# Six chunks of gathered rows among the one-hot groups, and another order of the embedding units

## The reference, cut to what matters

```python
hf = rms_norm(x, norm_ffn)
x = x + peer_ffn(hf, ...)      # 8 heads x 16 chosen experts of 16384 for each token
x = x + jax.nn.sigmoid(rms_norm(x, ple_norm) @ ple_w_gate) * (pe @ ple_w)
```

## Time and profile before

| | |
|---|---|
| median of 3 runs | 4200.87 us (4199.17 to 4205.4) |
| the profiled execution | 4196.88 us |
| its span | 4194.8 us |
| TensorE, VectorE, GpSimd busy | 89%, 63%, 44% of the span |
| data moved | 1063.93 MB, a mean of 254 GB/s |
| layer 0: one-hot groups, dense pairs, end | from 930, 1036 and 1957 us |
| layer 1: the same | from 3019, 3123 and 4046 us |

### The profile page before, as it was taken

One profiled execution on the slowest core, in us unless ns is written; L12 is line 12 of the kernel. 1 busy time (PEld: TensorE's weight loads), 2 busy tenths in 40 slices (PEclk: granted clock), 3 DMA queues, 4 the chain that ended last, 5 costly groups with the idle time before them and its releaser, 6 DMA issues. The chain is left out here.

```text
span 4194.8 us, 42902 instructions
## 1 busy us (share of the span) xinstructions
PE 3743.3 (89%) x15498; PEld 2766.4 (66%) x15498; DVE 2647.2 (63%) x5548; ACT 734.3 (18%) x1375; POOL 1860.7 (44%) x1714
## 2 busy tenths in 40 slices
PE   8889998978999999994797899989789999999937
PEld 7546787867666666651685467878676666666516
DVE  4766215748677676877657652167486777668776
ACT  2243302212000000000222433022120000000002
POOL 6101103776455455556371020047664554555563
PEclk9889999999999999997898999999899999999968
DMA  3201134548999999999722011445599999999997
GB/s 104 111 30 41 57 137 115 125 120 299 409 409 409 409 402 410 406 409 397 274 83 111 31 41 67 141 119 123 131 311 410 409 406 407 409 408 407 402 391 267
DMA packets 333955, 1063.93 MB, mean 254 GB/s; under 512 B 79152, under 2 KB 96176, under 8 KB 312496
## 3 DMA queue, kind: packets, MB, share of 16 engines
q0 software_dynamic: 184320, 537.08, 34.8%
q1 hardware_dynamic: 132368, 505.22, 31.9%
q10 hardware_dynamic: 17056, 18.88, 1.3%
HBM read 1025.27 MB, written 35.78 MB: 253 GB/s over the span
## 5 line engine op out<-in xcount | busy, mean ns | idle before, releaser
L1665 PE MATMUL bank<-v_tile,shared 128*128 128x512 f32 x2048 | 908.4, 598 | 38.5 <-DVE shared L2041 35.3
L2100 POOL DMA_INDIRECT u_rows<-in_peer_u,idx_all x512 | 645.1, 1260 | 591.9 <-DVE act_u L1998 478.2
L2010 DVE SCALAR_TENSOR_TENSOR x<-v_rows,act_w,x 128x1024 f32<-128x1024 f32 x512 | 657.7, 1285 | 335.2 <-DMA v_rows<-in_peer_v,idx_all 316.9
L2100 POOL DMA_INDIRECT v_rows<-in_peer_v,idx_all x512 | 561.7, 1097 | 423.4 <-DVE x L2010 331.7
L1998 DVE CUSTOM_DVE_ANT_0 u_rows<-u_rows,h 128x1024 f32<-128x1024 f32 x512 | 610.9, 1222 | 189.9 <-DMA u_rows<-in_peer_u,idx_all 187.5
L1665 PEld LDWEIGHTS bank<-v_tile,shared 128*128 128x128 f32 x2048 | 392.5, 192 | 493.1 <-issue 447.2
L2110 POOL DMA_INDIRECT first_cells<-first_gate,cell_all x256 | 417.1, 1629 | 578.5 <-DVEq L1990 462.4
L1653 PE MATMUL bank<-hT,bT 128*128 128x256 f32 x2048 | 452.5, 379 | 0.0
L1653 PEld LDWEIGHTS bank<-hT,bT 128*128 128x128 f32 x2048 | 388.4, 190 | 72.0 <-issue 22.0
L1557 PE MATMUL bank<-hT,ring 128*128 128x256 f32 x1536 | 341.1, 383 | 14.2 <-PEq L150 14.2
L1557 PEld LDWEIGHTS bank<-hT,ring 128*128 128x128 f32 x1536 | 293.6, 192 | 56.5 <-issue 15.8
(11 more groups left out here) (375 smaller groups left out, 4749.8 us busy)
## 6 DMA issues: line engine op xcount, KB each, us to landing
v_tile<-in_peer_v SPq DMA_DIRECT2D x256, 512.0 KB, 7.5
ring<-in_w_in_panels SPq DMA_DIRECT2D x76, 1024.0 KB, 4.9
bT<-in_peer_ut SPq DMA_DIRECT2D x128, 512.0 KB, 7.9
ring<-in_peer_w_query SPq DMA_DIRECT2D x32, 1024.0 KB, 5.2
aT<-in_peer_ut SPq DMA_DIRECT2D x64, 512.0 KB, 6.9
sT<-in_peer_ut SPq DMA_DIRECT2D x64, 512.0 KB, 6.8
ring<-in_ple_w_gate SPq DMA_DIRECT2D x24, 1024.0 KB, 6.8
first_cells<-zeros SPq DMA_DIRECT2D x16, 1024.0 KB, 11.1
```

Of the source, the lines that this page charges most:

```text
L1665: ins = mm(acc[t][part][:, :], act_pair[p % AHEAD][:, at:at + P], v_tile[:, e % DENSE, part * 512:part * 512 + 512], start=(e == 0), stop= ...
L2010: stt(out=m.x[:, 2 + t, :], in0=vr[:, n % RINGS, :], scalar=act_w[:, p % 4, i:i + 1], in1=m.x[:, 2 + t, :], op0=ALU.mult, op1=ALU.add).the ...
L2100: nc.gpsimd.indirect_dma_start(out=rows[:, n % RINGS, :], out_offset=None, in_=table, in_offset=bass.IndirectOffsetOnAxis(ap=idx_all[:, t, ...
```

## The change

`HOT_CHUNKS` goes from 4 to 6: chunks 0 to 5 lie behind one-hot groups 4, 9, 14, 19, 24 and 29, each with the `pre` that stood there now behind it; `query(1, 2)` moves with chunk 3 to group 19. Chunks 6 to 8 lie beside `pre(6)` to `pre(11)`. `DENSE_END` goes from 59 to 61, so the 64 pairs are spread over chunks 9 to 60, again 52 chunks. The units run in the order 1, 0, 2. The end of the list becomes

```diff
-HOT_CHUNKS = 4
+HOT_CHUNKS = 6
-DENSE_END = 59
+DENSE_END = 61
+LOADS_AT = 59
+SUMMED_AT = 65
...
-    after = {DENSE_END: [("add",), ("embed", 0)], DENSE_END + 1: [("scale", 0), ("turn", 0)], DENSE_END + 2: [("turned", 0)]}
-    for unit in range(2):
-        at = DENSE_END + 2 + 2 * unit
...
+    after = {LOADS_AT: [("load_ple",)]}
+    for unit, at in ((1, DENSE_END - 2), (0, DENSE_END)):
+        after.setdefault(at, []).extend([("add",), ("embed", unit)] if unit == 0 else [("embed", unit)])
+        after.setdefault(at + 1, []).extend([("scale", unit), ("turn", unit)])
+        after.setdefault(at + 2, []).append(("turned", unit))
         for n in range(4):
-            after.setdefault(at + n // 2, []).append(("embedded", unit, n))
-            after.setdefault(at + n // 2 + 1, []).append(("embedding", unit, n))
+            after.setdefault(at + 2 + (n // 2 if unit else 0), []).append(("embedded", unit, n))
+            if unit or n < 2:
+                after.setdefault(at + 3 + n // 2 if unit else SUMMED_AT, []).append(("embedding", unit, n))
...
-    order += [("sums",), ("embed", 2), ("scale", 2), ("turn", 2), ("turned", 2)]
+    order += [("sums",), ("embed", 2), ("scale", 2), ("turn", 2), ("turned", 2), ("embedding", 0, 2), ("embedding", 0, 3)]
...
+        idle = scores[:, :, :, :, :].rearrange("p a t s k -> p (a t s k)")
+        early_hT = idle[:, 0:D].rearrange("p (k n) -> p k n", k=KD)
+        early_sig = idle[:, D:2 * D].rearrange("p (n c) -> p n c", c=PANEL)
+        w_last = [a.rearrange("p a n -> p (a n)").rearrange("p (k c) -> p k c", c=PANEL) for a in (m.bT[:, 2:4, :], qry[:, :, :])]
...
-            if what[0] == "embedded":
+            if what[0] == "embedded" and what[1] == 1 and what[2] < RING:
...
-                w = panel()
+                if unit == 1 and n < RING:
+                    w_gate[n] = panel()
+                if unit == 1 and n == RING:
+                    pe.wait_ge(s.w_in, 16 * 2)
+                w = lambda k: w_gate[n][:, k, :] if n < RING else w_last[k // 4][:, k % 4, :]
...
-                bank = to_vec.open()
+                side = unit == 0 and n >= 2
+                bank = m.banks[4 + n] if side else to_vec.open()
...
-            def add():
+            def load_ple():
+                for _ in range(RING):
+                    panel()
                 sp.wait_ge(s.hot_filled, QUADS)
                 sp.dma_start(gain[:, :], io.ple_norm[bass.ds(layer, 1), :].partition_broadcast(P).rearrange("p l d -> p (l d)")).then_inc(s.p_in, 16)
                 sp.wait_ge(s.pre_done, KEYS)
                 sp.dma_start(pT, weight(io.p, layer, 0, 2, 0, T)).then_inc(s.p_in, 16)
                 for k in range(2):
                     sp.dma_start(w_ple[k], io.ple_w[layer, k * P:(k + 1) * P, :]).then_inc(s.p_in, 16)
+                sp.wait_ge(s.selected, PEER_HEADS)
+                for k in range(2):
+                    sp.dma_start(w_last[k], io.ple_w_gate[layer, RING][:, 4 * k:4 * k + 4, :]).then_inc(s.w_in, 16)
...
             def embedded(unit, n):
-                if unit:
-                    act.wait_ge(s.ple_added, 4 * unit + n - 3)
+                if unit == 2:
+                    act.wait_ge(s.ple_added, 4)
```

More of the change, by code:

```diff
@@ L1669, in turn @@
             def turn(unit):
-                if unit == 0:
+                if unit == 1:
                     pe.wait_ge(s.pre_read, PAIRS_ALL)
                 for t, tile in zip(unit_at(unit), UNITS[unit]):
-                    pe.wait_ge(s.ple_h, tile + 1)
+                    pe.wait_ge(s.ple_h, ple_rank[tile])
                     for part, banks in ((0, to_act), (1, to_vec)):
@@ L1677, in turn @@
                             kk = 4 * part + k
-                            ins = nc.tensor.transpose(bank[:, k * P:(k + 1) * P], ple_h[:, t, kk * P:(kk + 1) * P], m.c("ident"))
+                            ins = nc.tensor.transpose(bank[:, k * P:(k + 1) * P], normed_of(unit, t)[:, kk * P:(kk + 1) * P], m.c("ident"))
                         ins.then_inc(banks.filled, 1)
@@ L1688, in sums @@
                 ins.then_inc(s.last_sums, 1)
+            w_gate = {}
             def embedded(unit, n):
@@ L1698, in embedded @@
                     for k in range(KD):
-                        ins = mm(bank[:, cols(t)], ple_hT[:, k, t * P:(t + 1) * P], w[:, k, :], start=(k == 0), stop=(k == KD - 1))
+                        ins = mm(bank[:, cols(t)], turned_of(unit, t)[:, k, :], w(k), start=(k == 0), stop=(k == KD - 1))
                 ins.then_inc(s.act_filled, 1)
-                panels.released.append((s.act_filled, to_act.n))
                 if unit == 2:
                     return
-                bank = to_vec.open()
+                side = unit == 0 and n >= 2
+                bank = m.banks[4 + n] if side else to_vec.open()
                 for t, tile in zip(unit_at(unit), UNITS[unit]):
@@ L1761, in add @@
                     sp.dma_start(w_ple[k], io.ple_w[layer, k * P:(k + 1) * P, :]).then_inc(s.p_in, 16)
+                sp.wait_ge(s.selected, PEER_HEADS)
+                for k in range(2):
+                    sp.dma_start(w_last[k], io.ple_w_gate[layer, RING][:, 4 * k:4 * k + 4, :]).then_inc(s.w_in, 16)
             loads = iter(range(len(sources)))
-            parts = {"gate": panel, "mix": panel, "out": panel, "query": panel, "embedded": panel, "pre": pre, "first_gates": first_gates,
-                     "values": values, "add": add}
+            parts = {"gate": panel, "mix": panel, "out": panel, "query": panel, "pre": pre, "first_gates": first_gates,
+                     "values": values, "load_ple": load_ple}
             for what, *n in order:
@@ L1853, in embed @@
                 for t, tile in zip(unit_at(unit), UNITS[unit]):
-                    squares = h[:, 0, :] if unit == 2 else ple_h[:, t, :]
-                    step.step(f(squares, m.x[:, tile, :], ACT.Square, accum_out=pss[:, t:t + 1]))
-                    f(prms[:, t:t + 1], pss[:, t:t + 1], ACT.Sqrt, bias=m.c("eps"), scale=1.0 / D).then_inc(s.ple_rms, 1)
+                    squares = h[:, 0, :] if unit == 2 else normed_of(unit, t)
+                    step.step(f(squares, m.x[:, tile, :], ACT.Square, accum_out=stat(unit, t, 0)))
+                    f(stat(unit, t, 1), stat(unit, t, 0), ACT.Sqrt, bias=m.c("eps"), scale=1.0 / D).then_inc(s.ple_rms, 1)
             def turn(unit):
@@ L1870, in embedded @@
                 scale = prstd[:, unit_at(2)[0]:unit_at(2)[0] + 1] if unit == 2 else 1.0
-                f(ple_sig[:, n, at], bank[:, at], ACT.Sigmoid, scale=scale).then_inc(s.act_read, 1)
+                f(sig_of(unit, n), bank[:, at], ACT.Sigmoid, scale=scale).then_inc(s.act_read, 1)
                 sig_count[unit, n] = banks.n
@@ L2056, in scale @@
                         tt(ple_h[:, t, :], m.x[:, tile, :], gain[:, :], ALU.mult).then_inc(s.ple_h, 1)
-                        v.wait_ge(s.ple_rms, tile + 1)
+                        v.wait_ge(s.ple_rms, ple_rank[tile])
                         nc.vector.reciprocal(prstd[:, t:t + 1], prms[:, t:t + 1]).then_inc(s.last_scaled, 1)
                         continue
-                    v.wait_ge(s.ple_rms, tile + 1)
-                    step.step(nc.vector.reciprocal(prstd[:, t:t + 1], prms[:, t:t + 1]))
-                    stt(out=ple_h[:, t, :], in0=m.x[:, tile, :], scalar=prstd[:, t:t + 1], in1=gain[:, :],
+                    v.wait_ge(s.ple_rms, ple_rank[tile])
+                    step.step(nc.vector.reciprocal(stat(unit, t, 2), stat(unit, t, 1)))
+                    stt(out=normed_of(unit, t), in0=m.x[:, tile, :], scalar=stat(unit, t, 2), in1=gain[:, :],
                         op0=ALU.mult, op1=ALU.mult).then_inc(s.ple_h, 1)
@@ L2067, in turned @@
                     bank = banks.take()
-                    nc.vector.tensor_copy(ple_hT[:, 4:8, t * P:(t + 1) * P], bank[:, :].rearrange("p (k n) -> p k n", k=4)).then_inc(s.vec_read, 1)
+                    nc.vector.tensor_copy(turned_of(unit, t)[:, 4:8, :], bank[:, :].rearrange("p (k n) -> p k n", k=4)).then_inc(s.vec_read, 1)
             def embedding(unit, n):
```

26 lines of the change are left out of this document (15 added, 11 removed).

## The result

The changed kernel takes 4217.45 us (median of 7 runs) against 4200.35 us: a ratio of 1.004, 95% interval 1.003 to 1.005. It is slower by 17 us, where 4199 us and no change were forecast. Six of the seven runs lie at 4208.68 to 4221.95 us; the seventh, at 15079.51 us and a granted clock of 0.499, was a slow one and stays out of the ratio. The profiled execution has a span of 4220.2 us against 4194.8, so it shows 25 us where the medians show 17.

The account below looks back on a forecast made before the run. VectorE was taken to bound the front, bytes the middle, the chain between units the end. Layer 0: 11.6 - 1 + 2.6 - 14.9 = -1.7; layer 1: -0.2; together -1.9 on 4200.87, 4199 us, range 4186 to 4210.

Parts of the forecast that it names:

- front: First one-hot group to the start of the dense pairs: two more chunks make it 11.6 us (layer 0) and 13.1 us (layer 1) longer.
- end: Last chunks to the last addition: fewer chunks and units reordered make it 14.9 us shorter in each layer.
- middle: Dense pairs: same 64 pairs, 52 chunks and bytes per chunk, so 0 us; 1 us off per layer for earlier scatters.
- The larger of the two bounds counts, VectorE's, if the rows come in time: Front: growth by VectorE's work less waits, 11.6 and 13.1 us, outweighs growth by bytes, 0.0 and 2.4 us.
- middle, with the loads: Dense pairs: 1 us off for scatters ending earlier, 2.6 us added for loads, in each layer.
- free transfer time: Front: 18.3 us (layer 1) and 20.7 us (layer 0) free, against 20.7 us for the two chunks' 8.4 MB.
- The one-hot waits: Front: VectorE's waits for the one-hot product, 7.2 us in layer 1 and 8.7 in layer 0, all go.
- rival (b): Front: rows come late as GpSimd's 20.6 us a chunk passes VectorE's 18 to 23; +16 in all, 4215 us; chance 0.15.
- The lock: Front: VectorE instructions taking both ports lock out GpSimd's descriptor writing; growing with more fetches, it would work for rival (b).
- TensorE is not decisive: Middle: TensorE, busy 886.9 of 922.5 us, does not set the length; its last dense product waited 10.3 us for a gate product.
- Rival (a): Middle: TensorE sets it, its start slipping some 6 us less than VectorE's growth; total -14, 4187 us; chance 0.25.
- The loads: Embedding panels, four in place of twelve: one more MB in the full stretch adds 2.6 us a layer; the 6 MB burst is covered.

Follow-up runs that it names:

- e4: Kernel before with HOT_CHUNKS 6 alone, DENSE_END still 59 and the old end, so 50 chunks beside the pairs; 4237.63 us, ratio 1.0087.
- e12: e5 with a sixth chunk among the one-hot groups and late gates, 50 chunks beside the pairs; 4194.59 us, ratio 0.9984.
- e10: Kernel before with half of 16 v tiles not loaded in each layer, all engine work as it was; 4179.66 us against 4196.96.
- e8: Changed kernel with one of eight column blocks left out of the dense u products from pair 12 on; 4220.07 us, ratio 1.0052.
- e2: Changed kernel with HOT_CHUNKS back at 4, DENSE_END still 61 and the new end kept; 4218.17 us, ratio 1.0044.
- e3: Changed kernel with HOT_CHUNKS 4, DENSE_END 59 and LOADS_AT 57: old front, new end; 4209.29 us, ratio 1.0026.
- e5: e3 with the last two products of unit 0 two chunks later in the list; 4175.37 us, ratio 0.9942.
- e1: Changed kernel with GATES_AFTER 11 in place of 9, so the wait for the store no longer stands ahead of pre(10); 4211.58 us, ratio 1.0031.
- e9: Changed kernel with GATES_AFTER 11 and LOADS_AT 60: late gates, embedding loads behind the last pair's v tiles; 4212.66 us, ratio 1.004.
- e6: e5 with LOADS_AT 58, the 6 MB of embedding loads behind the last v tiles; 4176.74 us, ratio 0.9945.
- e7: Kernel before with one of eight column blocks left out of the dense u products from pair 12 on; 4208.02 us, ratio 1.0023.
- e11: e5 with a fifth chunk among the one-hot groups and first_gates behind pre(11); 4173.14 us, ratio 0.9948.

## Why the prediction was wrong

**The cause.** Twelve of the fourteen kernels of the table, which differ in front, end, SyncE's order and TensorE's work, need the bytes ahead of `add` over 391 to 395 GB/s. The two below that, 386 to 390 GB/s (e4, e12), are those with six chunks in the front and only 50 beside the pairs. An equal rate in many kernels shows little by itself. What carries the reading is that 4.2 MB a layer taken away, with all engine work left in place, gave 17 us back (e10), that 36 us of TensorE's work taken away gave nothing (e8), and that `DENSE_END` costs 23 to 28 us a layer (e2 against e3) while six chunks in the front cost what four do (the changed kernel against e2). The change takes two chunks out of the end, where they were nearly free (e5), and puts them ahead of `add`, where they cost 8.4 MB / 394 GB/s = 21.3 us; with the moved panel and what else slipped ahead, 9.1 and 9.8 MB are 23.1 and 24.9 us. Less the 14.9 and 16.1 us of a shorter end that leaves 8.2 and 8.8, 17 us in all, against 17 in the medians and 25 in the profiled pair.

**The step that failed** is the split of the price between front and middle. The two chunks were priced in the front alone, by VectorE's work less its waits ("The larger of the two bounds counts, VectorE's, if the rows come in time"), and then "The middle ... no change, 0 us". In us a layer:

| | forecast | measured |
|---|---|---|
| front | 11.6, 13.1 | 14.5, 16.7 |
| middle, with the loads | 1.6, 1.6 | 11.3, 10.8 |
| end | -14.9, -14.9 | -14.9, -16.1 |

Of the 24 us between forecast and measured, 19 lie in the middle, the stretch from the end of the front to `add`. Of layer 0's 11.3 us there, 2.0 MB more are 5 us: 1.05 MB is the panel, and the rest is what the front did not take, for it moved 7.1 MB more and not 8.4. The remaining 6 us are a rate of 403 in place of 406 GB/s. With the gates read late (e1) `add` came 3.8 and 5.0 us earlier, so the late store may be most of them; the times do not tell it from nothing.

Behind the 0 stood a reading of the front: 18.3 and 20.7 us of free transfer time, taken as something that 8.4 MB would fill. They did not. At 406 GB/s the front of layer 0 had (406 - 287)/406 x 106.2 = 31.1 us to spare before and (406 - 311)/406 x 120.7 = 28.2 after: 3 us of it were used. The sum that shows it could be had from the earlier trace rows: a chunk takes VectorE 10.13 us and brings 4.19 MB, which is 414 GB/s. In a stretch whose length is VectorE's, a chunk more adds about as much time as its bytes need at the full rate, and so uses none of the spare time. Only VectorE's own waits could be won, and over the whole stretch to `add` they were not.

This is a sum over the stretch, and not a full rate while VectorE works on a chunk. Rows are fetched ahead, and in the changed kernel's front of layer 1 the groups ahead of chunk 2 and chunk 2 itself show the reverse:

```profile
3067.71:3075.89 8.18, 5.17 (x36) 4.10 (x34) 8.18 (x27) 2.08 (x4) 6.96 (x5) 1.00 1.05 412
3075.89:3086.03 10.14, 8.04 (x40) 6.89 (x40) 9.79 (x15) 1.80 (x3) 8.01 (x8) 1.00 0.67 192
```

Over the six chunks of that front the mean is 275 GB/s, over its groups 335.

**The front's size.** 11.6 and 13.1 us forecast, 14.5 and 16.7 measured. The one-hot waits went, as said. In layer 1 VectorE is busy 19.9 us more (115.81 against 95.93), against 20.3 in the sum. But one wait for rows came in chunk 1, 2.4 us in layer 0 and 2.95 in layer 1. It is of rival (b)'s kind, at a single place, and is most of what the front grew beyond the forecast:

```profile
3061.07 1.23 DVE L2019 CUSTOM_DVE_ANT_0 u_rows<-u_rows,h 128x1024 f32<-128x1024 f32 x1 [2.95 <-DMA u_rows<-in_peer_u,idx_all]
```

GpSimd's fetches did not grow dearer: 50 of them took 1.29 us each in the changed front, 34 took 1.30 before. The lock of which the Trainium skill (SBUF — State Buffer, Who interferes with whom) tells did no more harm to a fetch with more fetches beside the groups.

**The middle and TensorE.** "TensorE is not decisive" was right: e8 takes 36 us of its work away and nothing moves. Rival (a) was wrong in its premise, and its sign too: I let TensorE start 6 us earlier than VectorE, while it waited 18.8 us behind the store. That wait was not named in the prediction at all. The three runs with it removed or made harmless (e1, e8, e9) put it at no more than 4 to 5 us a layer in the profiles, not told from nothing in the times. The two kernels that are slow to `add` beyond their bytes (e4, e12) are those where TensorE starts latest on the pairs and has the fewest chunks beside them; that this is why is inferred.

**The end.** -14.9 forecast, -14.9 and -16.1 measured. Unit 0's product runs in one piece, 9.06, 7.07 and 7.07 us with eight short matmuls each for its first three parts, and VectorE idles behind it:

```profile
4164.94 7.07 PE L1715 MATMUL bank<-ring,shared 128*128 128x256 f32 x32
...
4173.57 7.07 PE L1715 MATMUL bank<-ring,shared 128*128 128x256 f32 x32
...
4194.29 1.04 PE L1688 MATMUL bank<-consts,shared 128*128 128x128 f32 x8
```

```profile
4192.59 0.16 DVE L2079 RECIPROCAL small<-small 128x1 f32<-128x1 f32 x1 [16.19 <-ACT small L1877]
```

Those 16.2 us of VectorE are the two chunks' place: in e5 they stand there and the end is as long. I saw that "unit 0's 34.5 us of product ... now stands alone" and did not ask what else could lie beside it.

**The loads.** +2.6 forecast, 3.4 and 3.6 measured in e3. The burst of 6 MB holds the last pair 25 us and harms nothing (e6, e9).

**Open.** Why e7 became slower; why one execution of e10 gave back 2.5 us in layer 0 and 9.0 in layer 1; why the last store takes 30.5 us; and the 2.7 and 2.6 us by which the changed kernel's stretch to `add` exceeds its bytes.

The version to keep is e5 or e11: the new end with its products split around chunk 63, dense sums up to chunk 59, and four or five chunks among the groups, 0.5 to 0.6% faster than before. The two are not told apart.

## What to carry to other kernels

When a stretch behind a stage runs with full transfer engines, count the bytes from the start of the stage to the barrier and divide by the mean rate of the whole; free transfer time inside it is only used by work that brings more bytes than the full rate moves in the time by which that work makes the stage longer. Divide a step's bytes by the time that it adds (here 414 GB/s) and compare with the full rate before taking a gap in one stage as room for a step of another. Take bytes across the barrier into the stretch that is bound by something else: here two chunks cost 23 to 28 us a layer ahead of `add` and nothing behind it, once no gelu stood behind a sigmoid.

## What the runs showed of the hardware

The last 2 MB store of the gates took 30.46 us to land in layer 1 of the changed kernel, beside transfers at 411 GB/s. In the kernel before, the two stores of this kind of layer 0, of which the last had a DMA share of 1.09 beside it, took a median of 12.7 us (the view of transfers of that kernel from 930 to 1040 us; columns: out, in, queue, kind, count, KB each, median us to landing):

```profile
dense_gates<-gates ACTq DMA_DIRECT2D x2, 2048.0 KB, 12.7
```

With five chunks among the groups (e11) the last stores took 29.3 and 28.8 us, with six and late gates (e12) 38.5 and 34.4. What makes the difference is not shown.

The mean rate over a stretch of 1060 to 1095 us, in which gathers, dense tiles, gates and stores come in different orders, was 391 to 395 GB/s in twelve of fourteen kernels.
